# First-layer LayerNorm of a hybrid decoder kernel: scale and shift applied to the turned rows on ScalarE

## The reference

```
z = x @ w_in                      # 1024 -> 3592, four head groups
mix = concat(mLSTM, retention, RG-LRU, RWKV-7)(z) @ w_out
x = LN(ALPHA*x + mix)
x = LN(ALPHA*x + cross_attention(x, mem_k, mem_v))
x = LN(ALPHA*x + square(relu(x @ w_up)) @ w_down)
# LN(x) = (x - mean) * rsqrt(var + 1e-5) * g + b
```

## Time and profile before

| what | value |
|---|---|
| median of 3 runs | 2259.37 us (2255.07 to 2262.56) |
| the profiled execution | 2256.26 us |
| its span in the trace | 2254.4 us |
| TensorE matmul busy | 2199.6 us, 98% of the span |
| VectorE busy | 1173.6 us, 52% |
| ScalarE busy | 430.5 us, 19% |
| first matmul starts | 14.66 us |

### The profile page before, as it was taken

The page is one execution under the profiler, slowest core; times in us unless marked ns, Lnnn a source line. Parts: engine busy times, 40 slices in busy tenths (PEclk is TensorE's granted clock), DMA queues, the critical chain, the costliest instruction groups (busy, mean ns, idle before and its releaser), DMA issues. The chain is left out here.

```text
span 2254.4 us, 32268 instructions
## 1 busy us (share of the span) xinstructions
PE 2199.6 (98%) x13430; PEld 1616.0 (72%) x13430; DVE 1173.6 (52%) x2031; ACT 430.5 (19%) x915; POOL 115.4 (5%) x208
## 2 busy tenths in 40 slices
PE   7999999999999999999999999999999999999997
PEld 5877775547856888888888777655388478888885
DVE  5652236567366444775166422555755474447633
ACT  2332222021212211100023321321113022120000
POOL 0111101000000000000002111010001000000000
PEclk9999999999999999999999999999999999999998
DMA  7121014253542122222242111144236412232221
GB/s 266 71 75 40 26 43 115 88 178 129 189 168 94 59 91 75 75 75 78 72 133 75 38 40 59 48 118 143 82 150 225 150 57 75 76 108 78 75 75 40
DMA packets 136336, 217.28 MB, mean 96 GB/s; under 512 B 33672, under 2 KB 67776, under 8 KB 136064
## 3 DMA queue, kind: packets, MB, share of 16 engines
q1 hardware_dynamic: 133888, 211.02, 27.3%
q10 hardware_dynamic: 2304, 4.20, 0.5%
HBM read 198.39 MB, written 14.58 MB: 94 GB/s over the span
## 5 line engine op out<-in xcount | busy, mean ns | idle before, releaser
L730 PE MATMUL psum<-xT,ring 128*128 128x256 f32 (+1 forms) x768 | 222.1, 415 | 0.1
L2350 PE MATMUL psum<-tmp 128*128 128x272 f32 x768 | 181.2, 392 | 0.0
L2350 PEld LDWEIGHTS psum<-tmp 128*128 128x128 f32 x768 | 145.9, 190 | 30.1
L730 PEld LDWEIGHTS psum<-xT,ring 128*128 128x128 f32 x768 | 131.3, 189 | 35.2 <-issue 10.2
L680 PE MATMUL psum<-xT,ring 128*128 128x256 f32 (+1 forms) x512 | 122.4, 399 | 4.3 <-ACT big L1894 2.0
L727 PE MATMUL psum<-ring,ext 128*128 128x512 f32 x256 | 123.7, 620 | 0.0
L2444 PE MATMUL psum<-big,ring 128*128 128x256 f32 (+1 forms) x512 | 118.4, 393 | 0.0
L680 PEld LDWEIGHTS psum<-xT,ring 128*128 128x128 f32 x512 | 97.8, 193 | 26.4 <-issue 4.6
L2444 PEld LDWEIGHTS psum<-big,ring 128*128 128x128 f32 x512 | 97.0, 190 | 19.9 <-DMA ring<-in_w_down 0.2
L2350 PE MATMUL psum<-xT,ring 128*128 128x272 f32 x448 | 107.2, 392 | 0.0
L2350 PEld LDWEIGHTS psum<-xT,ring 128*128 128x128 f32 x448 | 85.0, 190 | 17.4
(11 more groups left out here) (517 smaller groups left out, 3733.6 us busy)
## 6 DMA issues: line engine op xcount, KB each, us to landing
ring<-in_w_down SPq DMA_DIRECT2D x16, 2048.0 KB, 7.7
ring<-in_w_in SPq DMA_DIRECT2D x14, 2048.0 KB, 8.4
ring<-in_w_up SPq DMA_DIRECT2D x14, 2048.0 KB, 7.6
big<-in_cache_mem_k SPq DMA_DIRECT2D x16, 1024.0 KB, 7.7
ring<-in_xa_wk SPq DMA_DIRECT2D x4, 2048.0 KB, 8.8
ring<-in_xa_wv SPq DMA_DIRECT2D x4, 2048.0 KB, 10.3
ring<-in_w_out SPq DMA_DIRECT2D x4, 2048.0 KB, 9.2
ring<-in_xa_wq SPq DMA_DIRECT2D x4, 2048.0 KB, 10.8
```

The lines of the kernel that those rows point to most:

```text
L730: ins = pe.matmul(bank[:, :c.stop - c.start], wring[:, n % 2, k, i * P:(i + 1) * P], xTv[:, k, c], start=(k == 0), stop=(k == KC - 1))
L2350: ins = pe.matmul(ps[:, :HT], left[:, k, :], right[:, k, :], start=(k == 0), stop=(k == KH - 1))
```

## The change

In the first layer only, the row tile is now normalised without gain and shift: `normal_rows` does the statistics, waits for `rstd`, and makes one pass `(x - mean) * rstd`, counted by a new semaphore `xhat`. TensorE turns tiles on `xhat` instead of `ln_done`. Gain and shift come as 16 rows of 128 (`gbr`, two small loads), are turned by TensorE into columns (`gbc`), and ScalarE applies them per feature block while it copies out of PSUM: 8 instructions a tile in place of 2, each with scale and bias read per partition.

The rows themselves, which are still needed for y and the residual, get gain and shift from `scaled_rows`: two passes a tile on VectorE, tiles 0 and 1 behind the last `normal_rows`, tiles 2 to 4 behind the fourth `zx_sum`. `ln_done` is now counted there.

The wait for slab 0 stands behind the turns of tiles 0 and 1. The two spread loads of gain and shift move in the SyncE queue from ahead of x tile 1 and slab 0 to behind the sample rows. In both layers the turns of `Sraw` (TensorE) and their copies (ScalarE) move behind `z_pair(1)`.

```diff
 turn_x_tensor:
-            pe.wait_ge(sig["ln_done"], 5 * ln + at + 1)
+            pe.wait_ge(sig["ln_done" if ln else "xhat"], 5 * ln + at + 1)
 turn_x_scalar:
+                if ln:
+                    ins = s.activation(xTv[:, 4 * g:4 * g + 4, t0:t0 + n], ps[:, :, :n], ACT.Copy)
+                else:
+                    for c in range(4):
+                        k = 4 * g + c
+                        ins = s.activation(xTv[:, k, t0:t0 + n], ps[:, c, :n], ACT.Identity, scale=gbc[:, k:k + 1], bias=gbc[:, KC + k:KC + k + 1])
+                bk.give(ins, ("xT", ln, T, g))
 head_tensor:
-                w = slab_pe(pe, 0)
                 if l == 0:
                     pe.wait_ge(sig["ident"], 16)
+                    pe.wait_ge(sig["gb"], 32)
+                    ps = bk.begin(pe, ("gb",), 4)
+                    bk.filled(pe.transpose(ps[:, :2 * KC], gbr[:2 * KC, :], ident[:2 * KC, :2 * KC]), ("gb",))
                     for T in range(2):
                         turn_x_tensor(pe, bk, sig, LN0, T, T, (2, 3))
+                w = slab_pe(pe, 0)
 head_scalar:
-                    for T in range(2):
-                        ln_scalar(s, sig, LN0, T, T)
+                    ln_scalar(s, sig, LN0, 0, 0)
+                    ps = bk.take(s, ("gb",))
+                    bk.give(s.activation(gbc, ps[:, :2 * KC], ACT.Copy), ("gb",))
+                    bk.given(s, ("gb",))
+                    ln_scalar(s, sig, LN0, 1, 1)
+            def normal_rows(v, T):
+                n = TILES[T][1]
+                x = xk[:n, T, :]
+                for half in range(2):
+                    ins = v.bn_stats(stats[:n, T, half, :], x[:, half * 512:half * 512 + 512])
+                v.wait_ge(sig["v"], sig.up(ins, "v"))
+                v.wait_ge(sig["ln_var"], sig.up(v.bn_aggr(mv[:n, T, :], stats[:n, T].rearrange("p a b -> p (a b)")), "ln_var"))
+                v.wait_ge(sig["ln_rstd"], T + 1)
+                sig.up(v.tensor_scalar(x, x, mv[:n, T, 0:1], rstd[:n, T:T + 1], ALU.subtract, ALU.mult), "xhat")
+            def scaled_rows(v, T):
+                n = TILES[T][1]
+                x = xk[:n, T, :]
+                v.wait_ge(sig["ln_param"], 32)
+                for g in range(2):
+                    bk.take(v, ("xT", LN0, T, g))
+                v.wait_ge(sig["v"], sig.up(v.tensor_tensor(x, x, lnp[:n, 0, :], ALU.mult), "v"))
+                sig.up(v.tensor_tensor(x, x, lnp[:n, 1, :], ALU.add), "ln_done")
 vector program:
                     head_vector(v)
+                    if l == 0:
+                        for T in range(2):
+                            scaled_rows(v, T)
...
                     zx_sum(v, 3)
+                    if l == 0:
+                        for T in range(2, 5):
+                            scaled_rows(v, T)
                     zw_sums(v, 1)
 tensor program:
+                    for u in (0, 1):
+                        z_pair(pe, u)
                     pe.wait_ge(sig["Sraw"], sig.at("Sraw", 16 * NB))
...
-                    for u in (0, 1):
-                        z_pair(pe, u)
```

More of the change, by code:

```diff
@@ L321, in turn_x_scalar @@
                 ps = bk.take(s, ("xT", ln, T, g)).rearrange("p (c t) -> p c t", c=4)
-                bk.give(s.activation(xTv[:, 4 * g:4 * g + 4, t0:t0 + n], ps[:, :, :n], ACT.Copy), ("xT", ln, T, g))
+                if ln:
[5 more added lines that the diff above has]
+                bk.give(ins, ("xT", ln, T, g))
         def ln_params(sp, sig, g, b):
@@ L474, in build @@
             dbase = region("tmp", 3072)
+            gbr = cols(tmp, dbase, P)
+            gbc = cols(tmp, dbase + P, 2 * KC)
             Xm = cols(tmp, dbase, H, CH)
@@ L792, in head_vector @@
                         v.wait_ge(sig[f"x{T}"], 16)
+                        normal_rows(v, T)
+                        continue
                     else:
@@ L803, in first_loads @@
                 sp.dma_start(con[:, :n_first], table[:, :n_first]).then_inc(sig.dma("ident"), 16)
-                ln_params(sp, sig, A["ln_in_g"], A["ln_in_b"])
+                for i, name in enumerate(("ln_in_g", "ln_in_b")):
+                    sp.dma_start(gbr[i * KC:(i + 1) * KC, :], A[name].rearrange("(c p) -> c p", p=P)).then_inc(sig.dma("gb"), 16)
                 sp.dma_start(xk[:, 1, :], xp[:, 1, :]).then_inc(sig.dma("x1"), 16)
@@ L809, in first_loads @@
                 sp.dma_start(xk[:NS, 4, :], A["x_sample"].rearrange("b t d -> (b t) d")).then_inc(sig.dma("x4"), 16)
+                ln_params(sp, sig, A["ln_in_g"], A["ln_in_b"])
                 first_slab(sp, 1, 0, sig.dma("first1"))
@@ L1896, in _ @@
                     head_scalar(s, z_half)
-                    for pr in range(2):
-                        ps = bk.take(s, ("SsT", pr))
-                        bk.give(act(SsT[:, pr].rearrange("p b v -> p (b v)"), ps, ACT.Copy), ("SsT", pr))
                     s.preload_act_table_set(LN_EXP)
@@ L1905, in _ @@
                     z_corner(1)
+                    for pr in range(2):
+                        ps = bk.take(s, ("SsT", pr))
+                        bk.give(act(SsT[:, pr].rearrange("p b v -> p (b v)"), ps, ACT.Copy), ("SsT", pr))
                     if l == 0:
```

## The result

The changed kernel took 2265.20 us against 2261.76 us for the one before, medians of 22 runs each (2259.84 to 2273.81, and 2253.14 to 2268.72). The ratio of the comparison is 1.0028 with an interval of 1.0017 to 1.0039: slower by 6.3 us, 3.8 to 8.8. The forecast was 10.1 us slower.

A forecast was written before the change was run, and what follows sets the result against it. TensorE, with matmuls in flight for 98% of the span, was taken to bound the kernel. Late rows 7.3, clock 2.1 and state turns 0.7 made 10.1 us on the 2259.37 median: 2269.5 us, +0.45%, range 2262 to 2275.5.

The forecast's parts named there:

- Direction and mechanism: SyncE queue: late sample rows' write delays parameter loads to 58.5, TensorE idles 8 to 9 us; slower, chance 0.77.
- The head, tiles 0 and 1: First layer's start: sixteen ScalarE copies at 0.37 us each; first product at 15.7 instead of 19.27, 3.6 us gained.
- Tile 4: Before the second four products: eight small copies, 2.6 us in all, give back 2.05 us of the lead, leaving 1.55.
- The rows of y: VectorE's late gain and shift passes delay write and parameter loads: `prow` turned at 61.1 instead of 53.8, +7.3 us.
- The clock: Behind the idle before `prow`: TensorE's granted clock falls to half, +2.1 us, bounds 0 and 3.4.
- State turns: Moved behind pair 1: nothing in the first layer, give or take 0.3; +0.7 us in the second, bounds 0 and 1.2.
- The sum: Whole kernel: 7.3 + 2.1 + 0.7 = 10.1 us slower, the head's gain inside the 7.3.
- three signs of being wrong: Wrong if `prow` is turned before 58, the granted clock stays full there, or the end moves less than `prow`.
- The clock holds: Rival at `prow`: cheap copies, shorter idle, no clock loss; about +6.0 us, 2265.4; chance 0.16.
- TensorE doesn't wait: Rival: parameter loads land before TensorE ends the head; -0.9 us, 2258.5, or 2252.9 if slab-bound; chance 0.05.
- The delay spreads: Rival: VectorE finishes slab 2's `zw_sums` late or the clock returns twice as slowly; 3 to 5 us more, 2273.5; chance 0.07.

The follow-up runs named there:

- rows first: Changed kernel with gain and shift of row tiles 2 to 4 done ahead of the four zx sums: 2255.05 against 2256.43 us, ratio 0.9992.
- The fill: Changed kernel with 12 needless 256-column matmuls on TensorE between the head and the wait for the parameter rows: 2265.73 against 2256.43 us, ratio 1.0029.
- loads first: Changed kernel with the 19 parameter loads queued ahead of the y writes, gain and shift kept elsewhere: 2260.40 against 2257.34 us, ratio 1.0009.
- both fills: Changed kernel with needless matmuls in the wait at row tile 4 (4) and before the parameter rows (12): 2266.26 against 2257.34 us, ratio 1.0036.
- combined version: Changed kernel with tiles 2 to 4 scaled before zx sums, VectorE copying second banks of tiles 0, 1, 4, state turns moved in first layer only: 2262.78 us, ratio 1.0013.
- again: The changed kernel run once more, unchanged: 2264.78 against 2257.34 us, ratio 1.0046; its profiled execution took 2274.81 us.
- tile 4 by VectorE: Changed kernel with row tile 4's second bank copied by VectorE in 4 tensor_scalar beside ScalarE's four copies: one run, 2271.91 us.
- state turns in one layer: Changed kernel with the state turns and their copies moved in the first layer only: one run, 2277.68 us.
- after: The changed kernel itself, first measured: 2265.20 against 2261.76 us for the kernel before, ratio 1.0028; its profiled execution took 2265.31 us.

## Why the prediction was right

**Direction and mechanism: right.** The sample rows' write came at 50.80 (forecast 51.7), the last load at 57.38 (58.5), and TensorE waited for it, without any such wait before. It idled 5.68 us, not the 8 to 9 forecast: it came through the head 1.15 later than reckoned (53.35 for 52.2), and `prow` was 2.07 earlier. Three experiments hang on this alone: two ways of having the loads early take the loss away, and one late write brings it about in the old kernel.

**The head, tiles 0 and 1: right, a little better.** First product at 15.21 against 15.7, sixteen copies in 5.68 us, 0.355 each against 0.37 in the sum. The copies, median 467 ns, answer to 0.46 in the text. This is where the page was weighed: the Trainium skill, "ScalarE: Activation LUTs", section "What ACT_TABLE_LOAD costs", makes such a copy 479 ns and, with its overlap, the spacing 386 ns. The trace has 467, and from start to start 348 ((5680 - 467) / 15), so here the copies are a little cheaper than by the page.

**Tile 4: right in its wait, blind to the clock.** Eight copies took 2.27 us (forecast 2.6) and TensorE waited 2.15. The head's lead was 2.31 us against 1.55. That the wait would halve the clock behind it (+1.69) wasn't foreseen: the lead at the end of the head was 0.45, not 1.55. It cost nothing at `prow`, since TensorE waited there for the loads anyway. That this term was left out did no harm is the luck of that wait: with the rows first, where none is left, it is what eats the gain.

**The rows of y: the mis-sized term.** Forecast +7.3 us at `prow`, measured +5.23 in the first trace, near the lower bound of 5.0. The sums started at 35.94, not 36.7, which gave 0.76, the queue from the write to the last load took 6.58 instead of 6.9, and the load landed and released TensorE 59.03 - 57.38 = 1.65 us after its issue, not 2.3. With the 0.3 that I had put behind the landing that is 0.76 + 0.32 + 0.95 = 2.03 of the 2.07. The 2.3 came from the earlier trace rows, loads of another size. Their median stayed 2.3 in the changed kernel: the mistake was to take them for this one. This part holds in every execution with a late write: 1.6 to 1.8 us from the last issue to `prow` in all eight. The start of the sums doesn't: in the seven of them made from the changed kernel it lies between 35.2 and 38.0, and `prow` between 58.4 and 61.1. So the +5.23 is one draw, and the second execution of the changed kernel had +7.32.

**The clock: right.** Forecast +2.1, measured 5.98 - 3.83 = +2.15, plus 0.28 for the two turns ahead of it. The fill gave back 2.0; the other 0.1 is no clock, since the pair takes 3.93 us at full clock too when it stands right behind the parameter turns. The Trainium skill, "TensorE: Matmul & The Clock Gate", section "HAM oscillation — how this bites in real kernels", has each wait for a transfer pay anew. The fall behind the 5.68 us wait agrees with it (2.15 us more), and the one behind the wait for ScalarE's copies is like it (1.69 us more), but the same 2.15 us wait was free in two other executions.

**State turns: first layer right, second layer low.** In the first layer the third pair came 0.5 later than `prow`, its two turns at half clock and the pair explain (8.15 - 5.23 - 0.28 - 2.15 = 0.49), above the 0.3 allowed: the eight turns took 0.92 us from their start to the next matmul in the old place and take 1.38 in the new one, where the memory rows' turns wait 0.34 for the state copies. The second layer cost 1.21, forecast 0.7, bound 1.2. There the order was right, with the table load behind the state copies. But the turns came 0.5 later than reckoned: with the layer's shift of 9.63 taken off, they start at 1191.50, not 1190.95, and the load ends at 1194.52, not 1194.05.

**The sum.** By the trace, 8.15 and 1.21 make 9.4 us for the 10.1 forecast: the rows 2 too dear, the state turns 1 too cheap. That the sum came nearer than its terms is luck. The rest, to the +9.1 of the spans, is what code that doesn't differ gained and lost on the way (+1.48 between the third pair and the second layer, and -1.7 behind its third pair).

**The times: partly open.** Medians of 6.3 and 10.4 us bracket the trace. The runs fall into groups by mean granted clock. The kernel before, 80 runs in the three later comparisons: 41 at 0.994 or more, median 2254.2; 32 at 0.990 to 0.993, 2261.8; 7 below, 2265.5. The changed kernel, 33 runs: 13 at 0.992 or more, median 2262.9; 12 at 0.990 or 0.991, 2265.3; 8 at 0.988, 2273.7. Best group against best group it is 8.7 us, middle against middle 3.6, worst against worst 8.2 (the half clock that the change itself brings lowers its means a little, so the groups aren't quite alike). So a median of a handful of runs depends on how many of each group it meets, more than on most terms above. Whether the change moves runs from one group to another wasn't settled, but one thing stands out: the changed kernel's last group, 8 of 33 runs at 2273.3 to 2274.8, has no counterpart among the 102 runs of the kernel before in these comparisons and the first, whose longest is 2269.34.

**The rivals.** "The clock holds" fell to the 5.98. "TensorE doesn't wait" fell to the wait of 5.7 us; its deciding point was a write before about 43, and with rows first, at 43.60, the wait is indeed gone: 6.6 us of issues and 1.65 to the release end at 51.8, and TensorE comes at 53.3. "The delay spreads" got its wait, 1.7 us of VectorE for slab 2 at 77.05, but TensorE's second pair kept its length: nothing spread. None of the three signs of being wrong came: `prow` at 59.03 is behind 58, the clock fell there, and the end moved by 9.1 us, more than `prow` did.

## What to carry to other kernels

Follow an in-order queue past the instruction you delay: what stands behind a write that waits is late by the same amount, and its slack (here 12 us) is the budget. TensorE, busy 98% of the span, paid for its wait of several microseconds twice, once in time and once in clock, so look for the gain of an early head at the next wait that a load ends. And when the same code varies by more than the change, measure the change at milestones of the trace and not by the end.

## What the runs showed of the hardware

**The same code varies by up to 11 us, by the clock alone.** From the first layer's third pair to the second layer's first product no kernel differs. It took 1043.2 to 1044.5 us in six executions (1043.96 with the loads first), 1045.03 before, 1046.5 in the first of the changed kernel, 1046.6 with both fills, 1051.0 in the combined version and 1054.1 to 1054.3 in three: again, tile 4 by VectorE, and state turns in one layer. The clock accounts for it: added up over the stretch, the share of the clock that wasn't granted makes 1.8 to 13.4 us, and the length less that is 1040.3 to 1041.4 in all thirteen. The window 450 to 460 in the second execution of the changed kernel:

```profile
450.00:460.00 10.00, 10.00 (x74) 6.00 (x74) 0.58 (x3) 0.00 (x0) 0.00 (x0) 0.50 0.00 0
```

It is at half clock though TensorE is busy all the time, and the next 10 us are at 0.52. The stretch begins behind a wait of 1.05 us for VectorE. Timeline of that execution, and then the same instructions with the loads first:

```profile
447.30 1.10 PE L1345 MATMUL psum<-tmp 64*64 64x4 f32 x32 [1.05 <-DVE big L1795]
...
461.04 3.78 PE L735 MATMUL psum<-ring,ext 128*128 128x512 f32 x4
```

```profile
435.80 1.10 PE L1347 MATMUL psum<-tmp 64*64 64x4 f32 x32 [1.05 <-DVE big L1797]
...
447.00 1.98 PE L736 MATMUL psum<-ring,ext 128*128 128x512 f32 x4
```

The wait is the same to 0.01 us, and one execution then runs 20 us at half clock, the other at full. What decides between them wasn't found.

**A wait of one length, two outcomes.** Behind the 2.15 us wait for row tile 4 the 64 records took 17.45 us in four executions (after, rows first, loads first, fill before `prow`) and 15.76 in two (again, state turns in one layer). The four are those whose first 32 records took 8.65 to 9.4 us, the two those with 10.09 and 10.15. It is a correlation over six executions and no more.

**The length of a start varies too.** The first 32 records took 8.53 us in one execution and 10.15 in another, 1.6 apart, with the work the same; where the clock had fallen behind a wait, the same records took 1.7 to 2.6 us more (64 records behind tile 4, 16 of the first pair).
